# Identity products in TensorE's waits at stage borders, and row stores issued from the attention stage

## The reference

```python
mod_l = (silu(c) @ ada_w[layer] + ada_b[layer]).reshape(bsz, N_MOD, 1, d)
h_lat = modulate(x_lat, norm1_g[layer], mod_l[:, 0], mod_l[:, 1])
y_lat, y_ctx = mixer_ab(...) if layer % 2 == 0 else mixer_cd(...)
x_lat = x_lat + mod_l[:, 2] * y_lat
h2_lat = modulate(x_lat, norm2_g[layer], mod_l[:, 3], mod_l[:, 4])
f = moe_ffn(h2, router_w, router_b, w_gate[layer], w_up[layer], w_down[layer])
x_lat = x_lat + mod_l[:, 5] * f
```

## Time and profile before

| what | us |
|---|---|
| median of 3 runs (lowest, highest) | 1564.25 (1564.12, 1567.12) |
| profiled execution | 1569.16 |
| its span, first to last instruction | 1567.3 |
| TensorE busy (matmul) in it | 1260.3 |
| VectorE busy | 601.1 |
| ScalarE busy | 391.9 |
| mean granted TensorE clock | 0.908 |
| DMA: bytes moved, mean rate | 507.65 MB, 324 GB/s |

### The profile page before, as it was taken

The page is one execution under the profiler, slowest core; times in us unless marked ns, Lnnn a source line. Parts: engine busy times, 40 slices in busy tenths (PEclk is TensorE's granted clock), DMA queues, the critical chain, the costliest instruction groups (busy, mean ns, idle before and its releaser), DMA issues. The chain is left out here.

```text
span 1567.3 us, 36654 instructions
## 1 busy us (share of the span) xinstructions
PE 1260.3 (80%) x14918; PEld 724.2 (46%) x14919; DVE 601.1 (38%) x1633; ACT 391.9 (25%) x821; POOL 32.9 (2%) x76
## 2 busy tenths in 40 slices
PE   4998979985899997867754599889798996766766
PEld 3445646553575554434422446645354553333333
DVE  2456665327222221211111548765643442222222
ACT  2273333213222222222211322633211111101101
POOL 0102020000000000000001000000000000000000
PEclk9998999997999998989987699979799998878888
DMA  9703988449899999999997530063899999999997
GB/s 357 265 9 113 328 293 319 166 171 383 357 403 428 430 428 429 429 429 429 428 428 297 199 108 1 1 270 129 350 401 425 428 429 429 429 428 428 429 428 329
DMA packets 82715, 507.65 MB, mean 324 GB/s; under 512 B 12965, under 2 KB 17378, under 8 KB 56018
## 3 DMA queue, kind: packets, MB, share of 16 engines
q1 hardware_dynamic: 76152, 489.21, 76.1%
q10 hardware_dynamic: 3306, 8.78, 1.5%
q0 software_dynamic: 3184, 8.63, 1.4%
HBM read 494.58 MB, written 12.01 MB: 323 GB/s over the span
## 5 line engine op out<-in xcount | busy, mean ns | idle before, releaser
L1703 PE MATMUL bank<-sb_ring,sb_scratch 128*32 128x256 f32 x2240 | 139.9, 405 | 53.1 <-DMA sb_ring<-in_moe_w_up 44.3
L1924 PE MATMUL bank<-sb_ring,sb_scratch 128*32 128x256 f32 x1664 | 117.8, 446 | 59.8 <-DMA sb_ring<-in_moe_w_up 55.2
L1789 DVE TENSOR_TENSOR sb_scratch<-sb_scratch,bank 128x128 f32<-128x128 f32 x50 | 14.4, 288 | 318.8 <-ACT sb_scratch L1742 318.8
L1703 PEld LDWEIGHTS bank<-sb_ring,sb_scratch 128*32 128x32 f32 x2240 | 78.0, 117 | 112.8 <-DMA sb_ring<-in_moe_w_up 40.8
L1746 ACT ACTIVATE sb_scratch<-bank 32x256 f32<-32x256 f32 x200 | 75.0, 375 | 163.0 <-PE bank L1718 161.2
L1924 PEld LDWEIGHTS bank<-sb_ring,sb_scratch 128*32 128x32 f32 x1664 | 62.0, 128 | 114.5 <-DMA sb_ring<-in_moe_w_up 55.2
L2009 DVE TENSOR_TENSOR sb_scratch<-sb_scratch,bank 128x128 f32<-128x128 f32 x38 | 10.9, 288 | 242.9 <-ACT sb_scratch L1965 242.9
L1674 PE MATMUL bank<-sb_h,sb_scratch 128*32 128x256 f32 x1632 | 99.4, 384 | 3.7 <-DVE sb_scratch L1776 3.3
L1965 ACT ACTIVATE sb_scratch<-bank 128x128 f32<-128x128 f32 x38 | 10.6, 278 | 366.7 <-PE bank L1924 366.7
L1924 PE MATMUL bank<-sb_scratch 128*32 128x256 f32 x768 | 56.9, 462 | 31.2 <-DMA sb_scratch<-in_moe_w_up 29.5
L1703 PE MATMUL bank<-sb_scratch 128*32 128x256 f32 x960 | 60.6, 409 | 22.1 <-DMA sb_scratch<-in_moe_w_up 19.3
(11 more groups left out here) (410 smaller groups left out, 1879.8 us busy)
## 6 DMA issues: line engine op xcount, KB each, us to landing
sb_ring<-in_moe_w_gate SPq DMA_DIRECT2D x40, 2048.0 KB, 26.6
sb_ring<-in_moe_w_up SPq DMA_DIRECT2D x40, 2048.0 KB, 31.2
sb_ring<-in_moe_w_down SPq DMA_DIRECT2D x39, 2048.0 KB, 33.2
sb_ring<-in_ada_w SPq DMA_DIRECT2D x21, 2048.0 KB, 13.5
sb_scratch<-in_moe_w_gate SPq DMA_DIRECT2D x20, 2048.0 KB, 27.4
sb_scratch<-in_moe_w_up SPq DMA_DIRECT2D x20, 2048.0 KB, 31.5
sb_scratch<-in_moe_w_down SPq DMA_DIRECT2D x20, 2048.0 KB, 33.1
sb_ring<-in_moe_w_gate SPq DMA_DIRECT2D x8, 1024.0 KB, 9.3
```

The costliest lines, as they stand in the source:

```text
L1703: last = nc.tensor.matmul(c.bank(1, 2, FQ)[MB * q:MB * q + MB, :, :], m.xt[:, k, :], m.gu[j][:, :, k, q * FQ:(q + 1) * FQ], start=k == 0, ...
L1789: v.tensor_tensor(m.hm, m.sg, c.ps[1][:, FQ:2 * FQ], ALU.mult).then_inc(hm_ready, 1)
L1924: last = nc.tensor.matmul(c.bank(1, 2, FQ)[MB * q:MB * q + MB, :, :], m.xt[:, k, :], m.gu[j][:, :, k, q * FQ:(q + 1) * FQ], start=k == 0, ...
```

## The change

A helper, `hold_clock(out, n)`, issues n products of the identity with itself, repeated along the columns, into a PSUM bank (`c.ps[b]`) that holds nothing at that time. They are put at these places: the first stage ahead of the fourth chunk's product (5 of 256 columns), the MLA stage behind the second tile's transposes (3 of 512), the attention of layer 1 ahead of each `turn(u)` of its first three pairs (1 each), the fronts of both layers around the router's small products, the combine stage ahead of either burst of transposes (7 and 5), and the end of the SSD stage (5). In the front of layer 0, six stand behind a new wait for the router's scores; in the combine stage each group stands behind a wait for `added`. The other part: the row stores at the end of the MLA stage are issued by SyncE at the start of layer 0's attention stage, behind the barrier, and their wait stands directly behind them.

```diff
--- before.py
+++ after.py
@@ -128,6 +128,13 @@
 
     def bank(self, b, *dims):
         return cut(self.ps[b], 0, *dims)
+
+    def hold_clock(self, out, n):
+
+        width = out.shape[1] // P
+        for _ in range(n):
+            self.nc.tensor.matmul(out.rearrange("p (a f) -> p a f", f=P), self.ident[:],
+                                  self.ident[:].unsqueeze(1).to_broadcast([P, width, P]), start=True, stop=True, skip_group_check=True)
@@ first_stage, TensorE
             product_of(2)
             turn(1, 3)
             turn_rows(2)
+            c.hold_clock(c.ps[1][:, 2 * P:4 * P], 5)
             product_of(3)
@@ mla_stage, SyncE
                 load(sp)
-            sp.wait_ge(ada_done, md.n)
-            md.store(sp, stored)
@@ mla_stage, TensorE
                 last.then_inc(query_turned, 1)
+                if t == 1:
+                    c.hold_clock(c.ps[0][:], 3)
@@ mla_stage, at the end
-    return stored, 16 * md.Q * len(md.segments)
+
+    def store_rows(sp):
+        md.store(sp, stored)
+        sp.wait_ge(stored, 16 * md.Q * len(md.segments))
+    return store_rows
@@ attention_stage, SyncE
-            if rows_stored:
-                sp.wait_ge(*rows_stored)
+            if store_rows:
+                store_rows(sp)
             if out:
                 out.load_gates(sp)
@@ attention_stage, TensorE
-                turn(2 * j)
-                turn(2 * j + 1)
+                for u in (2 * j, 2 * j + 1):
+                    if mask and j < min(out_after):
+                        c.hold_clock(c.ps[7][:], 1)
+                    turn(u)
@@ output_front_stage, TensorE
                 part_product(s)
+            c.hold_clock(c.ps[3][:], 1 if last_stream else 2)
             turn(last_tile)
             pe.wait_ge(taken, left)
+            c.hold_clock(c.ps[3][:], 1)
             part_product(last_stream)
...
+            else:
+                pe.wait_ge(scored, 1)
+                c.hold_clock(c.ps[7][:], 6)
...
+            spare = c.ps[1][:, 2 * P:4 * P] if m.summed else c.ps[7][:]
+            c.hold_clock(spare, 1 if m.summed else 2)
             pe.wait_ge(compared, 1)
...
+            c.hold_clock(spare, 2 if m.summed else 1)
             pe.wait_ge(placed, 1)
...
+            c.hold_clock(c.ps[0][:] if m.summed else spare, 2)
@@ combine_norm_stage, TensorE
             for s in streams:
+                pe.wait_ge(added, 1 if s == 0 else LT)
+                c.hold_clock(c.ps[0][:], (7, 5)[s])
                 for b in range(4):
@@ project_ssd_stage, TensorE, at the end
             last.then_inc(y_mean, 1)
+            c.hold_clock(c.ps[0][:], 5)
```

More of the change, by code:

```diff
@@ L2649, in program @@
         last_in = [c.sem(f"last_ada_w_in{j}") for j in range(3)]
-        rows_stored = mla_stage(c, m, late, used, [lambda sp, a=a: last.load_weights(sp, a, last_in[a]) for a in range(3)])
+        store_rows = mla_stage(c, m, late, used, [lambda sp, a=a: last.load_weights(sp, a, last_in[a]) for a in range(3)])
         wo_in = c.sem("ab_wo_in")
@@ L2659, in program @@
         attention_stage(c, units, m.qt, lambda h: m.kt[:, h, :], lambda h, k: m.v[:, k, h * VD:(h + 1) * VD],
-                        QK ** -0.5, m.attn_t, m.p, m.pt, QK, sp_work=loads, sp_end=lambda sp: load_expert(c, mo, sp, 0, 0), md=last, out=out, rows_stored=rows_stored, ada_in=last_in)
+                        QK ** -0.5, m.attn_t, m.p, m.pt, QK, sp_work=loads, sp_end=lambda sp: load_expert(c, mo, sp, 0, 0), md=last, out=out, store_rows=store_rows, ada_in=last_in)
         def first_weights(sp):
```

2 lines of the change are left out of this document (1 added, 1 removed).

## The result

In alternation on the same chip the changed kernel takes 1550.52 us (median of 7 runs, 1546.12 to 1556.97) and the kernel before 1566.33 us (7 runs, 1563.06 to 1567.58): a ratio of 0.9902, 95% interval 0.9883 to 0.9920, or 15.8 us. The forecast was 1545 us (1537 to 1555).

The account below looks back on a forecast made before the run. Weight bytes bound the two expert stages; the other some 690 us is a chain of stages with barriers. Terms sum to 21.6 us: 1547.6 us from the profiled execution, 1542.6 from the median; forecast the middle, 1545 us (1537.5 to 1555).

Parts of the forecast that it names:

- First stage: Fourth chunk's products, cold after a 2.56 us wait: five fills fit the wait and win 1.6 us, transposes behind included.
- MLA stage: After the first six transposes: three fills in a 3.31 us wait warm the products and transposes behind, 4.0 us.
- Row stores: Border from MLA to attention: issuing the stores behind the barrier wins 3.8 us, warm first score records 1.3 us more.
- Front of layer 0: Router's ranks, small products and gather before layer 0's experts run warm: 3.0 us, not hidden by the 4.6 us transfer pause.
- Combine stage: Fills ahead of both transpose bursts: second burst warm, 1.7 us, and the projection behind warm, 1.9 us; together 3.6 us.
- Rival 4: Transposes let the clock fall, so the projection and the products behind MLA's transposes start cold: 17.7 us gain, 1549 us; chance 0.10.
- SSD end and attention of layer 1: Five fills at the SSD stage's end and one ahead of each early turn: first three pairs end sooner, 2.3 us.
- Front of layer 1: Ranks, gather, slot rows and first products before layer 1's experts: 2.0 us, between holding and falling clock.
- The prediction's own mark: Sign named beforehand that would prove the forecast wrong: in the changed kernel's profile, TensorE is the last engine at a barrier.
- The term's other branch: Layer 1's front if the clock holds behind the sum-bank products: ranks, gather, slot rows and first products win 2.6 us.
- Rival 1: Clock falls again in the remaining waits of both fronts, combine stage and attention: 15.7 us gain, 1551 us; chance 0.23.

## Why the prediction was right, and where it wasn't

The direction and the range held. Between the two profiled executions the sum is 2.9 us off (21.6 against 18.7), and that closeness is in part luck: by the table, four parts came 7.6 us short and five 4.8 us long, most of both from where the clock happened to fall. Between the timed medians it is 5.8 us off (21.6 against 15.8). The forecast took the middle between the sum from the profiled execution (1547.6 us) and from a median of three runs (1542.6). Against the 1550.5 us measured, the first was the better base, but why is not shown: the profiled execution's granted clock, 0.908, was that of most executions of the kernel before (mean 0.909 over 47), so it had hardly more cold clock than they.

- **First stage** (1.6 us): right on the fourth chunk, 1.47 us. Not weighed was that the second chunk and the first products of `project_lru_stage` stand behind unfilled waits of 1.7 and 3.4 us and were warm in the profile of before by chance. Cold, they take 1.7 us more each. Where the second chunk was warm behind the fills, in the run with the old stores, the stage is 39.70 us long, 1.65 less than before, the term as predicted; where it was cold the stage took 40.62 us in the first profile of the changed kernel and 42.25 in the second.
- **MLA stage** (4.0): 3.8 by the run without the stores' move.
- **Row stores** (3.8 and 1.3): 3.7 at the border, nothing given back by the gates or the fourth chunk's load. In the first profile the score records bring 1.6 of attention's 3.2 us (up to the fourth group of output products, 78.7 us behind the first score instead of 80.3); the rest is a cold stretch further on (322.8 to 329.6 us before) that came later and shorter. Nor do the 1.3 us hold in general: in three of the eight profiles that have the fills and the moved stores the clock falls 6 us behind the first score, and attention takes 126.0 us instead of 122.0 to 122.4. Alone the move brought 0.7 us where 5.1 were summed.
- **Front of layer 0** (3.0): 2.9 us up to the first refill of the stream; the gather is half as long in seven of nine profiles and cold in two. The pause of the transfers, 4.6 us before, is down to some 1.4 us at a share of 0.10 in the first profile, so hardly more than one us is left to win there.
- **Combine stage** (3.6): 2.1 us up to the projection and the 1.9 of the projection among the SSD stage's 2.9 us; the last 1.0 us is a cold stretch inside the SSD stage (1019.1 to 1022.5 us in the kernel before) that isn't there. Rival 4 fell.
- **SSD end and attention of layer 1** (2.3): 3.3 us, of which 0.9 in the unfilled end (16 value records in 1.12 us instead of 1.98). What is left, 2.4, is the term; the run without the products ahead of the turns suggests that those in the SSD stage's end earn it.
- **Front of layer 1** (2.0): this is the step that failed, by 4.7 us in the whole line. The prediction saw that TensorE would wait over 3 us behind the warm sum-bank products and that "falls the clock there, the ranks and the weight rows are cold and the fills behind them longer", and priced this at "about 1 us" of gain left. It is a loss of 2.7 us: the prediction took the small products as cold, but not the identity products as longer than the waits they stand in, at three places in a row, the last at a barrier. In this term the product was nowhere charged at its cold price of 1.75 us (measured 1.9: the last two took 3.78). The prediction's own mark, TensorE last at a barrier, was the one that came. The term's other branch, 2.6 us if the clock holds, was right: in the run without the combine stage's products the clock held there, and the front and all behind it were 2.8 us shorter than before (0.5 and 2.3).

Rival 1 named the mechanism at this place and gave 1551 us, which is the measured median. That its number fits is luck: of its places the combine stage held its clock in both profiles of the changed kernel (2.0 and 2.1 us up to the projection, and the projection warm), layer 0's front held it in the first (3.5 us) and lost it in the second, and layer 1's front brought a loss of 2.7 us where the rival had a gain of 0.5.

## What to carry to other kernels

A filler is free only where it is shorter than the wait it stands in, and its length depends on the clock. What a filler that is too long costs depends on who waits behind it: the combine stage's seven started at the lower clock and took 9.1 us in a wait of some 8.3, without a loss at the stage's end (19.2 us from their start to the projection, as with transposes in their place), while layer 1's five cost 3 us where each product or the barrier behind them was waited for. So give a filler the price at the lower clock as well, and where that is longer than the wait, ask whether the clock can have fallen ahead of it. A first gap left open (here 3.06 us) turned all fillers behind it into cost: close the gaps in order, and put the least at a barrier. What a filler speeds up ahead of a wait makes that wait longer.

## What the runs showed of the hardware

Thirteen executions of the changed kernel differ by 16 us, 54 of the kernel before by 14, and the traces show where: the clock falls and rises at other points of the same work from one execution to the next. The mean granted clock recorded with each execution goes with its time: 0.901 for the slowest of the kernel before (1574.07 us) and 0.916 for its fastest (1560.38), 0.927 and 0.937 for the changed kernel's (1562.38 and 1546.12). Behind the wait of 0.78 us ahead of layer 1's scores it fell in two of the profiles and held in nine. One profile of a kernel is one draw of these: `project_lru_stage`, warm in the profile of before, was so in three of twelve. And transposes lifted the clock as fast as products did (5.7 us).
